# Moving the operands of TensorE by 64 bytes against the split weights, in a two-block transformer kernel

## The chip, the cores and the metric

One core of a Trainium2 chip runs the whole kernel. The time is the device time of one execution in microseconds (us); shown are medians of several runs, and one execution under the hardware profiler.

## What is computed

Two stacks of two layers each, on 256 tokens with 1024 features, in float32:

```
first block (256 latent and 256 context tokens, 512 in all):
  layer 0: modulated rmsnorm -> one projection to q, k, v and a gated branch
           -> neighbourhood attention + spatial gating -> projection -> residual
           rmsnorm -> conv FFN, inner width 2816 -> residual
  layer 1: the same frame with a retention mixer, then only the 256 latent tokens
second block (16 meta tokens + 256):
  layer 0: h + ab_mixer(rmsnorm(h))      # mLSTM and RG-LRU branches
           h + relu(rmsnorm(h) @ w1)^2 @ w2      # inner width 4096
  layer 1: h + differential attention, and the same MLP
  rmsnorm, without the 16 meta tokens
```

Nearly all of the arithmetic is `activations @ weights` with weight matrices that are each read once.

## The kernel before, in words

**Precision.** A float32 product is made of three fast passes. Every operand is split into a high part (rounded to the type float32r) and a low part (the rest). `project` (line 417) adds up high x high, low x high and high x low in PSUM; these are lines 456, 457 and 458. The activations are split where they are produced, by a norm or an activation function (`Hhi`/`Hlo`, `Fhi`/`Flo` and others); the weights are split as they arrive.

**Slots.** The weights come in slots of up to 1 MB (128 partitions x 2048 floats), listed in `PROJ`: `stream_weights` loads slot after slot from the sync queue into `w_raw[:, 0]` and `w_raw[:, 1]` in turn; ScalarE writes `w_hi` (`split_hi`, L383), VectorE writes `w_lo = w_raw - w_hi` (`split_lo`, L393), in two halves each; then TensorE uses the slot. Both have two buffers too, of 8 KB per partition, so one slot is prepared while the one before is used. The order of everything is written out by hand, with counted semaphores.

**Matmuls of a slot.** For most projections (`kind` "feat") the stationary operand is a 128 x 128 block of weights and the moving operand is one row of activations, that is 128 features x T tokens:

```
w = slice((k * p.C + c) * P, (k * p.C + c + 1) * P)
pe.matmul(o, w_hi[:, r, w], x_hi(k), start=k == 0, stop=False)
pe.matmul(o, w_hi[:, r, w], x_lo(k), start=False, stop=False)
mm = pe.matmul(o, w_lo[:, r, w], x_hi(k), start=False, stop=k == last)
```

T is 512 (`T1`) in layer 0 of the first block and in `ret_k`, 256 (`SEQ`) in the rest of its layer 1, in `c_outa`, `c_outb` and in the MLP of the last layer, and 272 (`T2`) in the rest of the second block. So a slot of 8 x 2 blocks is 48 matmuls, and one of 11 x 1 blocks (`ffn*_out*`) 33. For `kind` "tok" (`hyb_v*`, `ret_v`) the operands change places: 128 tokens of activations are stationary, 256 columns of weights move (lines 451 to 453). In the projections with a `fill` (`hyb_*`, `ret_g`, `ab_o`, `ab_gate`, `c_*`) small matmuls of the attention or of the recurrences stand between those of `project`.

**Which stages there are, and how many matmuls `project` issues in each:** `hyb_g` 96, `hyb_qk0` to `hyb_qk3` 48 each, `hyb_v0` and `hyb_v1` 96 each, `hyb_u` 96, `hyb_out` 192; `ffn0_in0` and `ffn0_in1` 528 each, `ffn0_out0` and `ffn0_out1` 264 each; `ret_k` 192, `ret_q` 192, `ret_v` 768, `ret_g` 384, `ret_out` 384; `ffn1_in0`, `ffn1_in1` 528 each, `ffn1_out0`, `ffn1_out1` 264 each; the `ab_*` stages 1584 in all; `mlp0_in0`, `mlp0_out0`, `mlp0_in1`, `mlp0_out1` 384 each; the `c_*` stages 768 in all; the four of `mlp1` 384 each. Together 11280 of TensorE's 13225 matmuls.

**Addresses.** All buffers are placed by hand (`at`, line 180 on): the address in a partition is `base` = 16512 plus the offset given. 16512 is 128 modulo 256. Modulo 256 the addresses before are: `w_hi` and `w_lo` 128 (each block of 512 bytes too); `X` 128; `Hhi512`, `Hhi256` and their `lo` 192, with rows of 2048 or 1024 bytes; `A`, the start of the working area, 64, and with it `Fhi512`, `Fhi256`, `rv_out` (moving operand of `ret_out`) and the outputs of the hybrid stage; `Hhi272` 128, `Fhi272` 64, `ABhi` 64, with rows of 1088 bytes = 4 x 256 + 64. The MLP of the last layer uses the 272 buffers with 256 columns of each row.

Of the kernel before, what the change touches and what calls it, by code (L numbers as in the profile page):

```python
# [171 lines left out]
def stack_kernel(nc, t, out, layers):  # L172
# [3 lines left out]
    with ctx:  # L176
# [92 lines left out]
        r_ctx = at("r_ctx", [P, 2, SEQ], A + 88 * KB)
        rq = at("rq", [P, 8, SEQ], A + 48 * KB)  # L270
        rg = at("rg", [P, 16, SEQ], A + 56 * KB)
        r_dist = at("r_dist", [P, 2, 2, SEQ], A + 72 * KB)
        r_dec = [at(f"r_dec{i}", [P, 4, SEQ], A + (76 + 4 * i) * KB) for i in range(2)]
        r_rope = at("r_rope", [P, 2, 2, SEQ], A + 80 * KB)
        r_e = at("r_e", [P, 2, SEQ], A + 84 * KB)
        r_rs = at("r_rs", [P, 2, SEQ], A + 86 * KB)
        r_sq = at("r_sq", [P, 2, SEQ], A + 90 * KB)
# [2896 lines left out]
```

## Time and profile before

| | |
|---|---|
| median of 3 runs | 2044.6 us (2042.35 to 2045.34) |
| the profiled execution, its own time | 2041.65 us |
| its span, first to last instruction | 2039.9 us |
| mean granted clock of TensorE | 0.983 |
| TensorE matmuls | 1938.5 us busy, 95%, 13225 |
| VectorE, ScalarE, GpSimd | 61%, 45%, 11% busy |
| HBM | 293.94 MB read, 145 GB/s over the span |

The profile is one execution. The busy time of TensorE is the union of its matmuls, which overlap: each lasts longer (in the records) than the distance to the start of the next. So the mean duration of a matmul is not what it costs; what it costs is the spacing of the starts, which is a stretch of time over the number of matmuls that start in it.

### The profile page before, as it was taken

The numbers are of one execution on the slowest core, as the hardware profiler recorded it, in microseconds if no ns is written. First come the engines' busy times: TensorE is split into PE (matmuls) and PEld (weight loads), VectorE is DVE, ScalarE is ACT, GpSimd is POOL, SyncE is SP. The second block draws the span as 40 slices with busy tenths as digits, with TensorE's granted clock in tenths as the row PEclk, the third lists the DMA queues.
The fourth block names the chain that finished last, engine by engine and source line by source line (L and its number), as shares of the span: only waits on it lengthen the run. The fifth ranks groups of instructions, "written<-read, shape, count | busy, mean of one in ns | idle before, by whom it ended". The sixth has DMA issues, their size and how long they took to land.

```text
span 2039.9 us, 33160 instructions
## 1 busy us (share of the span) xinstructions
PE 1938.5 (95%) x13225; PEld 1709.0 (84%) x13225; DVE 1251.0 (61%) x1853; ACT 920.6 (45%) x1438; POOL 217.7 (11%) x171
## 2 busy tenths in 40 slices
PE   4999989999999899999979998999999999989998
PEld 3776647778887479999979997998899999879997
DVE  6355466543654556678577767656975567787564
ACT  4344344322332242158465554347554444565353
POOL 2100104430542000011000000000010010000001
PEclk8999989999999899999999999999999999999999
DMA  8611464433222523223435544532444544224553
GB/s 357 229 69 63 164 228 165 167 125 111 83 90 85 206 83 128 101 83 104 145 136 170 208 162 142 174 137 83 139 171 167 177 174 145 94 94 170 186 182 124
DMA packets 43950, 296.78 MB, mean 145 GB/s; under 512 B 4976, under 2 KB 6128, under 8 KB 11696
## 3 DMA queue, kind: packets, MB, share of 16 engines
q1 hardware_dynamic: 36576, 247.48, 35.0%
q10 hardware_dynamic: 6048, 42.50, 5.9%
q0 software_dynamic: 1200, 5.02, 0.7%
q8 instruction: 90, 1.47, 0.3%
q14 instruction: 36, 0.29, 0.0%
HBM read 293.94 MB, written 1.05 MB: 145 GB/s over the span
## 4 chain that ended last, share of the span: by engine, by line
PE 83%; DVE 8%; ACT 4%; DMA 3%; issue 1%; POOL 1%; SPq 0%; ACTq 0%; DVEq 0%; POOLq 0%
PE acc L456 23%; PE acc L457 22%; PE acc L458 22%; DVE w_lo L393 2%; PE acc L451 2%; PE wk L550 2%; PE acc L453 2%; PE acc L452 2%; PE wk L1672 1%; DMA ada_first<-in_w_ada 1%; DMA ada_ring<-in_w_ada 1%; ACT w_hi L383 1%; PE wk L730 1%; PE acc L1661 1%; PE wk L1401 1%
## 5 line engine op out<-in xcount | busy, mean ns | idle before, releaser
L456 PE MATMUL acc<-Hhi,w_hi 128*128 128x272 f32 (+2 forms) x2304 | 740.5, 321 | 29.4 <-DVE Hlo L772 10.1
L457 PE MATMUL acc<-Hlo,w_hi 128*128 128x272 f32 (+2 forms) x2304 | 717.9, 312 | 0.0
L458 PE MATMUL acc<-Hhi,w_lo 128*128 128x272 f32 (+2 forms) x2304 | 717.5, 311 | 0.0
L393 DVE TENSOR_TENSOR w_lo<-w_raw,w_hi 128x1024 fp32r<-128x1024 f32 (+2 forms) x472 | 575.5, 1258 | 183.9 <-ACT w_hi L383 182.4
L383 ACT ACTIVATE w_hi<-w_raw 128x1024 fp32r<-128x1024 f32 (+2 forms) x472 | 452.3, 1005 | 432.9 <-PE acc L458 339.6
L456 PEld LDWEIGHTS acc<-Hhi,w_hi 128*128 128x128 f32 x2304 | 437.1, 190 | 79.7 <-issue 42.0
L457 PEld LDWEIGHTS acc<-Hlo,w_hi 128*128 128x128 f32 x2304 | 437.4, 190 | 22.1
L458 PEld LDWEIGHTS acc<-Hhi,w_lo 128*128 128x128 f32 x2304 | 436.5, 189 | 23.0
L456 PE MATMUL acc<-Fhi,w_hi 128*128 128x256 f32 (+2 forms) x864 | 265.1, 307 | 2.8 <-DVE w_lo L393 1.5
L458 PE MATMUL acc<-Fhi,w_lo 128*128 128x256 f32 (+2 forms) x864 | 264.6, 306 | 0.0
L457 PE MATMUL acc<-Flo,w_hi 128*128 128x256 f32 (+2 forms) x864 | 264.3, 306 | 0.0
L456 PEld LDWEIGHTS acc<-Fhi,w_hi 128*128 128x128 f32 x864 | 162.9, 189 | 12.6 <-issue 2.2
L458 PEld LDWEIGHTS acc<-Fhi,w_lo 128*128 128x128 f32 x864 | 162.7, 188 | 8.0
L457 PEld LDWEIGHTS acc<-Flo,w_hi 128*128 128x128 f32 x864 | 162.4, 188 | 7.9
L1047 ACT ACTIVATE cgu<-acc,vec 128x512 f32<-128x512 f32 x44 | 34.2, 779 | 127.6 <-PE acc L458 127.6
L451 PE MATMUL acc<-w_hi,Hhi 128*128 128x256 f32 x320 | 91.6, 286 | 0.0
L453 PE MATMUL acc<-w_hi,Hlo 128*128 128x256 f32 x320 | 88.7, 277 | 0.0
L452 PE MATMUL acc<-w_lo,Hhi 128*128 128x256 f32 x320 | 88.7, 277 | 0.0
L1069 DVE SCALAR_TENSOR_TENSOR cgu<-acc,vec,cgu 128x510 f32<-128x510 f32 x44 | 32.6, 743 | 90.5 <-ACT cgu L1047 90.5
L976 ACT ACTIVATE sq<-Y 128x512 f32<-128x512 f32 (+1 forms) x32 | 16.4, 523 | 120.9 <-DVE Y L958 61.1
L1906 DVE TENSOR_TENSOR X<-acc,X 128x272 f32<-128x272 f32 (+3 forms) x48 | 20.4, 434 | 75.1 <-PE acc L458 75.1
L958 DVE COPY Y<-acc 128x256 f32 (+3 forms) x32 | 17.9, 558 | 77.5 <-PE acc L458 77.4
(393 smaller groups left out, 2426.6 us busy)
## 6 DMA issues: line engine op xcount, KB each, us to landing
w_raw<-in_w_ffn_in SPq DMA_DIRECT2D x44, 1024.0 KB, 4.9
ada_ring<-in_w_ada ACTq DMA_DIRECT2D x40, 1024.0 KB, 4.9
w_raw<-in_w_mlp_in SPq DMA_DIRECT2D x32, 1024.0 KB, 4.9
w_raw<-in_w_mlp_out SPq DMA_DIRECT2D x32, 1024.0 KB, 4.9
w_raw<-in_w_ffn_out SPq DMA_DIRECT2D x32, 704.0 KB, 4.1
ada_first<-in_w_ada SPq DMA_DIRECT2D x8, 1024.0 KB, 18.4
w_raw<-in_w_ret_v SPq DMA_DIRECT2D x8, 1024.0 KB, 4.9
w_raw<-in_w_ret_g SPq DMA_DIRECT2D x8, 1024.0 KB, 4.8
```

Of the source, the lines that this page charges most:

```text
L383: act.activation(w_hi[:, r, a:b], w_raw[:, r, a:b], ACT.Copy).then_inc(hi_done, 1)
L393: dve.tensor_tensor(w_lo[:, r, a:b], w_raw[:, r, a:b], w_hi[:, r, a:b].bitcast(F32), ALU.subtract).then_inc(lo_done, 1)
L451: pe.matmul(o, x_hi(k)[:, toks], w_hi[:, r, w], start=k == 0, stop=False)
L452: pe.matmul(o, x_hi(k)[:, toks], w_lo[:, r, w], start=False, stop=False)
L453: mm = pe.matmul(o, x_lo(k)[:, toks], w_hi[:, r, w], start=False, stop=k == last)
L456: pe.matmul(o, w_hi[:, r, w], x_hi(k), start=k == 0, stop=False)
L457: pe.matmul(o, w_hi[:, r, w], x_lo(k), start=False, stop=False)
L458: mm = pe.matmul(o, w_lo[:, r, w], x_hi(k), start=False, stop=k == last)
L550: mm = pe.matmul(wk[b:b + 32, bank, 0:256], cvec[:, k, 30 - 2 * j:62 - 2 * j], w[:, k * 256:(k + 1) * 256], start=first and k < 4, stop=la ...
L1047: act.activation(cgu[:, r, c, 0:n], acc_tile(p, r, c), ACT.Identity, bias=Vd("conv_b", m + layer * 44), scale=Vd("conv_w", m + (layer * 3 ...
L1069: dve.scalar_tensor_tensor(seqs(o, 1, SEQ), seqs(acc_tile(p, r, c), 0, SEQ - 1), w, seqs(o, 1, SEQ), ALU.mult, ALU.add).then_inc(conv_left, 1)
L1906: ins = dve.tensor_tensor(x, acc_tile(p, st.parity(), c), x, ALU.add)
```

## The change

It changes addresses and one row length, and no instruction. `w_hi` and `w_lo` begin 64 bytes further (192 modulo 256). `X` and the `H` area move up by 256, `A` becomes a multiple of 256 (128 modulo 256 as an address). Then, modulo 256: `Hhi512`/`Hlo512` and `Fhi512`/`Flo512` and the hybrid's outputs lie at 128; `Hhi256`, `Fhi256`, `Fhi272` and `rv_out` at 192; `Hhi272` still at 128 and `ABhi` at 128 with rows of 1088 bytes. The rows of `Fhi272`/`Flo272` become 1152 bytes = 4 x 256 + 128. The norm ahead of the retention (j == 2) writes to `R_hi`/`R_lo`, rows of 512 tokens that begin at 192; `ret_k`, `ret_q`, `ret_v` and `ret_g` read them. The other buffers of the retention move by 64 against `A`.

```diff
-        w_hi = at("w_hi", [P, 2, SLOT], 16 * KB, F32R)
-        w_lo = at("w_lo", [P, 2, SLOT], 32 * KB, F32R)
-        X = at("X", [P, DC, T1], 48 * KB)
+        w_hi = at("w_hi", [P, 2, SLOT], 16 * KB + 64, F32R)
+        w_lo = at("w_lo", [P, 2, SLOT], 32 * KB + 64, F32R)
+        X = at("X", [P, DC, T1], 48 * KB + 256)
         HB = 4352 * 4
-        h0 = 64 * KB
+        h0 = 64 * KB + 256
...
-        A = (at_const[0] + 127) // 128 * 128 + 64
-
-        H_hi = {T1: at("Hhi512", [P, DC, T1], h0 + 64, F32R), SEQ: at("Hhi256", [P, 16, SEQ], h0 + 64, F32R),
+        A = (at_const[0] + 255) // 256 * 256
+
+        H_hi = {T1: at("Hhi512", [P, DC, T1], h0, F32R), SEQ: at("Hhi256", [P, DC, SEQ], h0 + 64, F32R),
                 T2: at("Hhi272", [P, 16, T2], h0, F32R)}
-        H_lo = {T1: at("Hlo512", [P, DC, T1], h0 + HB + 64, F32R), SEQ: at("Hlo256", [P, 16, SEQ], h0 + HB + 64, F32R),
+        H_lo = {T1: at("Hlo512", [P, DC, T1], h0 + HB + 256 + 0, F32R), SEQ: at("Hlo256", [P, DC, SEQ], h0 + HB + 256 + 64, F32R),
                 T2: at("Hlo272", [P, 16, T2], h0 + HB, F32R)}
+
+        R_hi, R_lo = at("Rhi", [P, DC, T1], h0 + 64, F32R), at("Rlo", [P, DC, T1], h0 + HB + 256 + 64, F32R)
...
-        F_hi = {T1: at("Fhi512", [P, FFH, T1], A + 16 * KB, F32R), SEQ: at("Fhi256", [P, FFH, SEQ], A + 16 * KB, F32R),
-                T2: at("Fhi272", [P, MLH, T2], A + 16 * KB, F32R)}
+        F_hi = {T1: at("Fhi512", [P, FFH, T1], A + 16 * KB, F32R), SEQ: at("Fhi256", [P, FFH, SEQ], A + 16 * KB + 64, F32R),
+                T2: at("Fhi272", [P, MLH, 288], A + 16 * KB + 64, F32R)}
...
-        rv_out = at("rv_out", [P, 4, 2048], A + 16 * KB, F32R)
+        rv_out = at("rv_out", [P, 4, 2048], A + 16 * KB + 64, F32R)
...
-                act.activation(H_hi[n][:, c, 0:n], n32[:, c % 2, 0:n], ACT.Copy).then_inc(hhi_ready, 1)
+                hi = R_hi if j == 2 else H_hi[n]
+                act.activation(hi[:, c, 0:n], n32[:, c % 2, 0:n], ACT.Copy).then_inc(hhi_ready, 1)
...
-            ret = (lambda k: H_hi[T1][:, k, LAT:T1], lambda k: H_lo[T1][:, k, LAT:T1])
-            project(pe, "ret_k", *hyb, need=h_need(pe, 2))
+            both = (lambda k: R_hi[:, k, :], lambda k: R_lo[:, k, :])
+            ret = (lambda k: R_hi[:, k, LAT:T1], lambda k: R_lo[:, k, LAT:T1])
+            project(pe, "ret_k", *both, need=h_need(pe, 2))
```

(`F_lo` changes as `F_hi` does, the low half of the norm as the high half, and `ret_v` takes `both` as well.)

## Rows read from the trace of the kernel before

**Rows 1.** The page: busy time by engine, and the chain that ended last
```profile
PE 1938.5 (95%) x13225; PEld 1709.0 (84%) x13225; DVE 1251.0 (61%) x1853; ACT 920.6 (45%) x1438; POOL 217.7 (11%) x171
...
PE 83%; DVE 8%; ACT 4%; DMA 3%; issue 1%; POOL 1%; SPq 0%; ACTq 0%; DVEq 0%; POOLq 0%
PE acc L456 23%; PE acc L457 22%; PE acc L458 22%; DVE w_lo L393 2%; PE acc L451 2%; PE wk L550 2%; PE acc L453 2%; PE acc L452 2%; PE wk L1672 1%; DMA ada_first<-in_w_ada 1%; DMA ada_ring<-in_w_ada 1%; ACT w_hi L383 1%; PE wk L730 1%; PE acc L1661 1%; PE wk L1401 1%
```

**Rows 2.** Waits of TensorE, longest first: us in total, times, longest
```profile
engine line waited for: us in total, times, longest us
PE wk L859 <- DVE sq_acc L899: 18.0, 1, 18.0
PE wk L550 <- DMA ada_ring<-in_w_ada: 12.1, 8, 3.1
PE acc L456 <- DVE Hlo L772: 10.1, 3, 4.5
PE acc L456 <- DVE Hlo L802: 7.8, 5, 5.6
...
PE acc L456 <- DVE w_lo L393: 4.2, 7, 0.9
```

**Rows 3.** Busy time by window, stretches of matmul behind matmul only
```profile
core 0: us, PE busy (x) PEld busy (x) DVE busy (x) ACT busy (x) POOL busy (x), PEclk, DMA share, GB/s
236.98:242.82 5.84, 5.84 (x27) 4.70 (x25) 0.90 (x2) 2.35 (x4) 1.49 (x2) 1.00 0.66 247
443.89:498.26 54.37, 54.37 (x235) 43.57 (x234) 17.38 (x21) 10.85 (x14) 0.00 (x0) 1.00 0.35 121
498.26:619.12 120.86, 120.86 (x530) 99.16 (x529) 68.47 (x64) 43.14 (x53) 55.49 (x30) 1.00 0.26 88
627.58:681.01 53.43, 53.43 (x231) 43.05 (x229) 19.89 (x22) 14.51 (x21) 7.11 (x6) 1.00 0.34 113
729.11:761.85 32.74, 32.74 (x144) 26.86 (x143) 12.33 (x14) 5.89 (x6) 0.00 (x0) 1.00 0.38 129
...
761.85:783.61 21.76, 21.76 (x193) 21.76 (x192) 12.75 (x16) 9.33 (x9) 0.00 (x0) 1.00 0.46 153
981.82:1021.16 39.34, 39.34 (x335) 39.34 (x335) 20.21 (x22) 16.23 (x21) 4.10 (x6) 1.00 0.56 187
1109.24:1135.33 26.09, 26.09 (x231) 26.09 (x231) 15.57 (x22) 10.05 (x14) 0.00 (x0) 1.00 0.65 220
1135.33:1197.52 62.19, 62.19 (x530) 62.19 (x529) 49.20 (x84) 38.11 (x62) 0.00 (x0) 1.00 0.51 176
1202.77:1229.74 26.97, 26.97 (x231) 26.97 (x230) 15.15 (x22) 13.01 (x21) 4.08 (x6) 1.00 0.62 209
1546.25:1594.67 48.42, 48.42 (x386) 48.42 (x385) 23.22 (x26) 17.16 (x18) 0.00 (x0) 1.00 0.49 175
1892.16:1937.59 45.43, 45.43 (x386) 45.43 (x385) 23.05 (x26) 17.11 (x18) 0.00 (x0) 1.00 0.54 185
```

**Rows 4.** TensorE by line and form: ret_q, ffn1_in1, ffn0_in1
```profile
line engine op names shapes xcount | busy us, mean ns | idle before us <-releasers
L456 PE MATMUL acc<-Hhi,w_hi 128*128 128x256 f32 x63 | 17.4, 276 | 0.0
...
L457 PE MATMUL acc<-Hlo,w_hi 128*128 128x256 f32 x171 | 47.9, 280 | 0.0
L458 PE MATMUL acc<-Hhi,w_lo 128*128 128x256 f32 x171 | 47.7, 279 | 0.0
...
L457 PE MATMUL acc<-Hlo,w_hi 128*128 128x512 f32 x168 | 66.2, 394 | 0.0
L456 PE MATMUL acc<-Hhi,w_hi 128*128 128x512 f32 x168 | 65.9, 392 | 0.0
L458 PE MATMUL acc<-Hhi,w_lo 128*128 128x512 f32 x168 | 65.2, 388 | 0.0
```

**Rows 5.** TensorE by line and form, 800 to 870 us, inside ret_v
```profile
L451 PE MATMUL acc<-w_hi,Hhi 128*128 128x256 f32 x191 | 53.9, 282 | 0.0
L453 PE MATMUL acc<-w_hi,Hlo 128*128 128x256 f32 x191 | 52.8, 276 | 0.0
L452 PE MATMUL acc<-w_lo,Hhi 128*128 128x256 f32 x191 | 52.8, 276 | 0.0
```

**Rows 6.** VectorE and ScalarE by line and form, whole execution
```profile
L393 DVE TENSOR_TENSOR w_lo<-w_raw,w_hi 128x1024 fp32r<-128x1024 f32 x400 | 507.5, 1308 | 159.6 <-ACT w_hi L383 158.6
...
L383 ACT ACTIVATE w_hi<-w_raw 128x1024 fp32r<-128x1024 f32 x400 | 400.7, 1049 | 384.1 <-PE acc L458 298.9 <-PE acc L453 77.1 <-DMA w_raw<-in_w_ffn_in 6.2
```

More of the change, by code:

```diff
@@ L231, in stack_kernel @@
         ada_ring = at("ada_ring", [P, 2, SLOT], nt0 + 18 * KB)
-        ada_rows = [at("ada_rows0", [P, 2, 256], A + 32 * KB), at("ada_rows1", [P, 1, 256], h0 + 16 * KB + 64)]
+        ada_rows = [at("ada_rows0", [P, 2, 256], A + 32 * KB), at("ada_rows1", [P, 1, 256], h0 + 16 * KB + 128)]
         sq2 = at("sq2", [P, 2, T2], A + 85 * KB)
@@ L239, in stack_kernel @@
         last = at("last", [P, DC, SEQ], h0)
-        F_hi = {T1: at("Fhi512", [P, FFH, T1], A + 16 * KB, F32R), SEQ: at("Fhi256", [P, FFH, SEQ], A + 16 * KB, F32R),
-                T2: at("Fhi272", [P, MLH, T2], A + 16 * KB, F32R)}
-        F_lo = {T1: at("Flo512", [P, FFH, T1], A + 38 * KB, F32R), SEQ: at("Flo256", [P, FFH, SEQ], A + 38 * KB, F32R),
-                T2: at("Flo272", [P, MLH, T2], A + 38 * KB, F32R)}
+        F_hi = {T1: at("Fhi512", [P, FFH, T1], A + 16 * KB, F32R), SEQ: at("Fhi256", [P, FFH, SEQ], A + 16 * KB + 64, F32R),
+                T2: at("Fhi272", [P, MLH, 288], A + 16 * KB + 64, F32R)}
+        F_lo = {T1: at("Flo512", [P, FFH, T1], A + 38 * KB, F32R), SEQ: at("Flo256", [P, FFH, SEQ], A + 38 * KB + 64, F32R),
+                T2: at("Flo272", [P, MLH, 288], A + 38 * KB + 64, F32R)}
         cgu = at("cgu", [P, 2, 2, T1], A + 60 * KB)
@@ L266, in stack_kernel @@
         ro = at("ro", [P, 8, 2, SEQ], A)
-        rv = at("rv", [P, 4, 2048], A + 16 * KB)
-        rv_out = at("rv_out", [P, 4, 2048], A + 16 * KB, F32R)
[L269 to L277, printed above, removed]
+        rv = at("rv", [P, 4, 2048], A + 16 * KB + 64)
+        rv_out = at("rv_out", [P, 4, 2048], A + 16 * KB + 64, F32R)
+        r_ctx = at("r_ctx", [P, 2, SEQ], A + 88 * KB + 64)
+        rq = at("rq", [P, 8, SEQ], A + 48 * KB + 64)
+        rg = at("rg", [P, 16, SEQ], A + 56 * KB + 64)
+        r_dist = at("r_dist", [P, 2, 2, SEQ], A + 72 * KB + 64)
+        r_dec = [at(f"r_dec{i}", [P, 4, SEQ], A + (76 + 4 * i) * KB + 64) for i in range(2)]
+        r_rope = at("r_rope", [P, 2, 2, SEQ], A + 80 * KB + 64)
+        r_e = at("r_e", [P, 2, SEQ], A + 84 * KB + 64)
+        r_rs = at("r_rs", [P, 2, SEQ], A + 86 * KB + 64)
+        r_sq = at("r_sq", [P, 2, SEQ], A + 90 * KB + 64)
         qk = at("qk", [P, 16, T2], A)
@@ L771, in lo @@
                 dve.wait_ge(hhi_ready, DC * j + c + 1)
-                dve.tensor_tensor(H_lo[n][:, c, 0:n], n32[:, c % 2, 0:n], H_hi[n][:, c, 0:n].bitcast(F32),
+                hi, lo = (R_hi, R_lo) if j == 2 else (H_hi[n], H_lo[n])
+                dve.tensor_tensor(lo[:, c, 0:n], n32[:, c % 2, 0:n], hi[:, c, 0:n].bitcast(F32),
                                   ALU.subtract).then_inc(h_ready, 1)
@@ L3002, in _ @@
             pe_ada_close(pe, ADA_RING)
-            ret = (lambda k: H_hi[T1][:, k, LAT:T1], lambda k: H_lo[T1][:, k, LAT:T1])
-            project(pe, "ret_k", *hyb, need=h_need(pe, 2))
+            both = (lambda k: R_hi[:, k, :], lambda k: R_lo[:, k, :])
+            ret = (lambda k: R_hi[:, k, LAT:T1], lambda k: R_lo[:, k, LAT:T1])
+            project(pe, "ret_k", *both, need=h_need(pe, 2))
             pe.wait_ge(s_mod, 9)
             project(pe, "ret_q", *ret)
-            project(pe, "ret_v", *hyb, after=lambda s: (all_freed(pe, "ret_q") if s == 0 else None,
+            project(pe, "ret_v", *both, after=lambda s: (all_freed(pe, "ret_q") if s == 0 else None,
                                                         pe_rope(pe, rope_items(), [2 * s, 2 * s + 1], SEQ, swap_ret, 0)))
```

## The prediction

> **What bounds the kernel now.** I read the page first. TensorE is busy 95% of the span, and the chain that ended last is 83% TensorE [rows 1]. The three matmul lines of `project` (L456, L457, L458) alone are 67% of that chain: for every row of activations one matmul with the high weights, one with the low activations, one with the low weights. The list of waits says how little stands between them: TensorE's longest wait is one of 18.0 us in the first norm, all its waits for L393's `w_lo` are 4.2 us, and the DMAs of the weights that `project` streams do not appear [rows 2]. So the time is a number of matmuls times the spacing of their starts, and the question is whether a new address changes a spacing.
>
> No row of the page gives a spacing, so I took stretches in which matmul follows matmul and divided their length by the matmuls that start in them (the count of the row, less one or two that are in flight at an edge; by the code 528 in `ffn0_in1`, 192 in `ret_q`, 384 in `mlp0_out0`) [rows 3]. 512 columns: 120.86/528 = 228.9 ns in `ffn0_in1`; 54.37/233 = 233.3 in `ffn0_out0` and 53.43/229 = 233.3 in `ffn0_out1`; 32.74/143 = 228.9 in `ret_k`; 5.84/25 = 233.6 in `hyb_out`. 256 columns: 21.76/192 = 113.3 in `ret_q`, 26.09/230 = 113.4 in `ffn1_out0`; 62.19/528 = 117.8 in `ffn1_in1`, 26.97/229 = 117.8 in `ffn1_out1`, 39.34/334 = 117.8 in `ret_out`; 45.43/384 = 118.3 in `mlp1_out0`. 272 columns: 48.42/384 = 126.1 in `mlp0_out0`. The granted clock is 1.00 (the 2.4 GHz level) in all of them, so it is not the clock. At one column a cycle they would be 213.3, 106.7 and 113.3 ns. The lines by form repeat it: a matmul of 256 columns lasts 276 ns in `ret_q` and 279 to 280 in `ffn1_in1`, one of 512 lasts 388 to 394 in `ffn0_in1` [rows 4].
>
> What differs between stretches of one width is where the moving operand lies against the weights. Addresses are the base of 16512 plus the offset; modulo 256 the weights lie at 128. `Hhi512` and `Hhi256` lie at 192: I call that distance 64. `Fhi` and the hybrid's outputs lie at 64: distance 192. Buffers with rows of 1088 bytes move on by 64 with every row: rotating. The 512-wide spacing follows the distance in every stretch: 228.9 at 64, 233.3 at 192. The 256-wide one holds one of two values at either distance (113.3 or 117.8), and 118.3 when it rotates. I take 113.3 (and 226.7, 120.4 in proportion to the columns) as the floor; the rest is a collision of the two reads of TensorE, the moving rows and the next weights. Other engines are hardly in it: `ret_q` stays on its floor with VectorE at work for 12.75 of 21.76 us.
>
> **Against that, a rule.** The measured fact is that 256 columns take 113.3 ns in one stretch and 117.8 in another at one clock [rows 3]. The Trainium skill, "SBUF — State Buffer", section "Who interferes with whom", says that PE and ACT never wait on anyone and gives the moving operand and the weight load a read port each; by it no placement matters and the sum below would be zero. The trace does not agree about the spacing, but it does not show that addresses are the cause either, since one distance has both values. So it stays a rival.
>
> **The change part by part.** No instruction, wait or DMA is added, removed or reordered. What changes is the distance. All counts are from the code.
>
> 1. Wide rows of the hybrid and of `ffn0_in` (96 + 192 + 96 + 1056 = 1440 matmuls): weights at 192, rows at 128, so distance 64 becomes 192. If only the distance counts they take on the spacing of `ffn0_out0`: 1440 x (233.3 - 228.9) = +6.3 us. Bound below: the floor, 1440 x (226.7 - 228.9) = -3.2. I take +6.3, since the nearest rows are the same instruction at that distance.
> 2. Wide rows of `hyb_out` and `ffn0_out` (720): 192 before and after, 0; bounds 720 x (226.7 - 233.3) = -4.8 and 0. `ret_k` (192) goes from 64 to 0, which no wide row shows: 0, bounds -0.4 and +0.8.
> 3. Narrow rows put at distance 0. `ffn1_in` 1056 at 117.8, `ret_g` and `ret_out` 768 at 117.8, `ffn1_out1` 264 at 117.8; `ffn1_out0` 264 and `ret_q` 192 are at the floor; `ret_v` (768, with weights as the moving operand) is there by its durations, 276 ns for two of its three lines (L451's 282 hold the restarts behind the rope matmuls) [rows 5]. No stretch stays at distance 0. Best: all on the floor, (1056 + 768 + 264) x 4.45 = -9.3. Worst that a steady stretch of this width shows: all at 117.8, so 264 x 4.4 = +1.2 for `ffn1_out0`, 192 x 4.5 = +0.9 for `ret_q`, 768 x (280 - 276) = +3.1 for `ret_v`: +5.2. I take -9.3: a fixed distance is the only thing found on the floor (in three stages of it), and the rotating rows never are. This is the weakest step.
> 4. `F` of the second block gets rows of 1152 bytes instead of 1088: the four distances become two, 0 and 128, in turn. Best -768 x (126.1 - 120.4) = -4.4 and -768 x (118.3 - 113.3) = -3.8, so -8.2; worst, as the rotation but without its better rows, +1. I take half of the best, -4.1.
> 5. `H272` still rotates over all four distances, only beginning at another: 0. `hyb_v` (192): 0. The split of the weights on ScalarE and VectorE, 1049 and 1308 ns for 1024 elements [rows 6], reads and writes other addresses: 0, because it is hidden behind the matmuls and TensorE waits 4.2 us in all for it. A slot of 48 matmuls lasts at least 5.4 us (48 x 113.3 ns), and its two halves keep VectorE for 2.6 and ScalarE for 2.1 us; if these became 10% slower it would be 0.3 us of that slack. A faster TensorE needs its weights sooner, but `ffn1_out0` runs on the floor while the DMA engines are at 0.65, so that cover holds [rows 3].
>
> Sum: +6.3 + 0 - 9.3 - 4.1 = -7.1 us. The profiled execution took 1.8 us more than its span, 2041.65, and lies 2.95 under the median of 2044.6; so 2034.5 for such an execution and **2037.5** for the median.
>
> **The rivals.**
> - *The wide rows gain as well.* Everything goes to the floor: -3.2 - 4.8 - 9.3 - 8.2 = -25.5, 2019.1 us. For it: the wide stages show matmuls of 388 ns among those of 392 and 394, so the floor exists there [rows 4]. Against: distance 192 is measured, at 233.3, in three stages.
> - *Slower: distance 192 for the wide rows, and no floor for the narrow.* The place is `ffn0_in` and the hybrid's input, the price +6.3, and it decides as soon as steps 3 and 4 give back less than 6.3 us, 47% of the 13.4 that I count on. With all narrow rows at 117.8 and step 4 at 0 it is +6.3 + 5.2 = +11.5, 2056.1 us. For it: `ffn1_in1`, `ffn1_out1` and `ret_out` sit at 117.8 at two different distances, so a fixed distance is no promise; if it is how a stage is entered that chooses, the floor of `ret_q` and `ffn1_out0` can be lost.
> - *No effect.* The spacing comes from something else that the addresses do not touch: 2044.6. For it: two values at one distance. Against: the wide rows keep 228.9 and 233.3 apart by distance without exception.
>
> **How the numbers follow.** A measurement of this kernel can tell about 0.2%, 4.1 us, from no change. Forecast (narrow rows gain, wide rows pay) 0.32; wide rows gain as well 0.18; no effect 0.13; slower 0.35; the last 0.02 is a balance of gain and loss inside 0.2%. Faster is the first two, 0.50; same 0.15; slower 0.35. The forecast's own range is 2033 (step 4 gives all of its 8.2) to 2046 (step 3 gives half, step 4 nothing). The range given takes in the slower case with the upper bounds of `ret_k` and step 4 (2056.1 + 0.8 + 1 = 2058) and reaches down to 2021, most of the way to the full gain at 2019; what lies beyond both ends is the rest of that rival and a few chances in a hundred above, together under 2 in 10.
>
> **What would show it.** In the changed profile the count of TensorE's matmuls is the same, 13225. Step 1: `ffn0_in1` at 233.3 ns (123.2 us for the stretch that took 120.86). Step 3: `ffn1_in1` at 113.3, 59.8 us for 62.19; `ret_g`'s durations 276 instead of 280. Step 4: `mlp0_out0` between 120.4 and 126.1, so 46.2 to 48.4 us, and `mlp1_out0` below 45.43. `ab_qk` at its old 126.1. The forecast is wrong if `ffn1_in1` stays at 62 us, if `ffn0_in1` is shorter than before, or if stretches of one stage and one distance change with no order.

## The result, and the profile after

The changed kernel takes 2058.9 us (median; 2056.9 to 2060.11), the kernel before 2044.26 beside it: ratio 1.0078, 95% interval 1.0064 to 1.0092 (the two medians alone give 1.0072). It is slower by 0.8%, outside the range given (2021 to 2058) and on the side of the rival "slower". The profiled execution took 2059.26 us with a span of 2057.5, 17.6 more than the span before.

The page of the changed kernel: busy time, and the chain that ended last (two source lines were added above `project`, so L456 to L458 are now L458 to L460). They answer to [rows 1].

```profile
PE 1957.9 (95%) x13225; PEld 1724.5 (84%) x13225; DVE 1252.9 (61%) x1853; ACT 921.3 (45%) x1438; POOL 217.7 (11%) x171
...
PE 84%; DVE 8%; ACT 4%; DMA 3%; issue 1%; POOL 1%; SPq 0%; DVEq 0%; ACTq 0%; POOLq 0%
PE acc L458 23%; PE acc L460 22%; PE acc L459 22%; DVE w_lo L395 2%; PE acc L453 2%; PE acc L455 2%; PE acc L454 2%; PE wk L552 2%; DMA ada_first<-in_w_ada 1%; PE wk L1676 1%; ACT w_hi L385 1%; DMA ada_ring<-in_w_ada 1%; PE wk L732 1%; PE acc L1665 1%; PE wk L1405 1%
```

TensorE is busy 19.4 us longer with the same 13225 matmuls; VectorE went from 1251.0 to 1252.9 us, ScalarE from 920.6 to 921.3. The waits of TensorE (us in total, times, longest) name the same causes as [rows 2], each within some 2 us of what it was, and the one for `w_lo` is a little shorter:

```profile
engine line waited for: us in total, times, longest us
PE wk L863 <- DVE sq_acc L903: 17.9, 1, 17.9
...
PE acc L458 <- DVE w_lo L395: 3.6, 6, 0.9
```

So nothing new is waited for, and the matmuls themselves stand further apart. Busy time by window, in the same stages as [rows 3] (stretch and its length, then busy time and count of each engine, granted clock, DMA share, GB/s); in order `ffn0_out0`, `ffn0_in1`, `ret_k`, `ret_q`, `ret_out`, and then `ffn1_out0`, `ffn1_in1`, `mlp0_out0`, `mlp0_in1`, `mlp1_out0`:

```profile
core 0: us, PE busy (x) PEld busy (x) DVE busy (x) ACT busy (x) POOL busy (x), PEclk, DMA share, GB/s
447.41:501.78 54.37, 54.37 (x234) 43.80 (x233) 17.36 (x21) 10.87 (x14) 0.00 (x0) 1.00 0.35 121
501.78:624.98 123.20, 123.20 (x529) 99.26 (x528) 68.34 (x64) 43.15 (x53) 55.36 (x30) 1.00 0.25 87
725.23:766.08 40.85, 40.85 (x181) 33.70 (x180) 18.69 (x27) 13.41 (x18) 0.00 (x0) 1.00 0.30 103
766.08:789.11 23.03, 23.03 (x193) 23.02 (x192) 12.75 (x16) 9.32 (x9) 0.00 (x0) 1.00 0.45 144
992.25:1032.32 40.07, 40.07 (x335) 40.07 (x335) 20.21 (x22) 16.22 (x21) 4.12 (x6) 1.00 0.54 185
...
1121.11:1148.71 27.60, 27.60 (x232) 27.60 (x231) 15.71 (x22) 10.04 (x14) 0.00 (x0) 1.00 0.60 208
1148.71:1212.07 63.36, 63.36 (x531) 63.36 (x530) 49.10 (x83) 38.11 (x62) 0.00 (x0) 1.00 0.49 173
1561.24:1609.88 48.64, 48.64 (x387) 48.64 (x386) 23.22 (x26) 17.16 (x18) 0.00 (x0) 1.00 0.49 173
1609.88:1658.30 48.42, 48.42 (x386) 48.42 (x385) 30.12 (x46) 23.74 (x30) 0.00 (x0) 1.00 0.51 175
1910.21:1955.44 45.23, 45.23 (x386) 45.23 (x385) 23.05 (x26) 17.12 (x18) 0.00 (x0) 1.00 0.53 186
```

Divided by the matmuls that start in them: `ffn0_in1` 123.20/528 = 233.3 ns (228.9 before), `ffn0_out0` 54.37/233 = 233.3 as before, `ret_k` 40.85/180 = 227.0 (228.9). And at 256 columns `ret_q` 23.03/192 = 120.0 (113.3), `ret_out` 40.07/334 = 120.0 (117.8), `ffn1_in1` 63.36/528 = 120.0 (117.8), `ffn1_out0` 27.60/230 = 120.0 (113.4). `mlp0_out0` 48.64/384 = 126.7 (126.1), `mlp1_out0` 45.23/384 = 117.8 (118.3), and `mlp0_in1`, whose rows still rotate, 48.42/384 = 126.1.

**Where the 17.6 us are.** For each stage I took the mean start-to-start time of the matmuls that follow one another without a pause, in both traces, and multiplied the difference by the stage's matmuls:

| part | matmuls | predicted, us | by measured spacing, us |
|---|---|---|---|
| 1. wide, distance 64 to 192 | 1440 | +6.3 | +5.8 |
| 2. wide, 192 to 192; `ret_k` 64 to 0 | 912 | 0 | -0.4 |
| 3. narrow, to distance 0 | 3312 | -9.3 | **+11.8** |
| 4. rows that alternate 0 and 128 | 1536 | -4.1 | +0.1 |
| 5. `hyb_v`, 64 to 192, and all the rest | 4080 | 0 | +0.3 |
| sum | 11280 | -7.1 | +17.6 |

That the sum is the difference of the spans to the digit is partly luck, because two things outside the table cancel. The pauses of the two norms ahead of `ffn0_in0` and `ret_k` are 2.3 us shorter in the changed execution, and `c_outa` and `c_outb` last 2.6 us longer. For `c_outb`, the kernel before and then the changed one:

```profile
1831.11:1843.97 12.86, 11.59 (x97) 11.42 (x97) 10.24 (x13) 6.58 (x12) 0.90 (x2) 1.00 0.62 220
1847.22:1861.98 14.76, 13.50 (x97) 13.32 (x97) 10.22 (x13) 6.98 (x12) 0.89 (x2) 0.86 0.53 189
```

That is the clock, 1.00 against 0.86, and it does not take the change: a second trace of the kernel before (`before_again`, below) has `c_outb` at 14.63 us and 0.86 as well, and its span, 2044.2, is only 13.3 us under the changed one. By the starts of the stages the changed execution is 15.4 us behind when `c_outa` begins, and the medians are 14.6 apart. So my estimate from these is that the addresses cost about 15 us, nearly all of it in the spacing of parts 1 and 3.

Nor do the other engines cause it, although their writes of `w_hi` and `w_lo` moved too: in `ffn1_in1` of the changed kernel all 527 spacings are 120 ns to the nanosecond of the trace, while VectorE is busy for 49.10 of the 63.36 us and ScalarE for 38.11, so a spacing is the same whether they are at work or not.

### The profile page after: what moved, and what is told of

The parts are those of the page before. It is cut to its first block, busy times and chain, and to the rows that moved or that the text cites. A ratio compares the mean times of both kernels' runs of the same rounds, so it can differ in the third digit from the quotient of the medians.

```text
span 2057.5 us, 33160 instructions
## 1 busy us (share of the span) xinstructions
PE 1957.9 (95%) x13225; PEld 1724.5 (84%) x13225; DVE 1252.9 (61%) x1853; ACT 921.3 (45%) x1438; POOL 217.7 (11%) x171
## 4 chain that ended last, share of the span: by engine, by line
PE 84%; DVE 8%; ACT 4%; DMA 3%; issue 1%; POOL 1%; SPq 0%; DVEq 0%; ACTq 0%; POOLq 0%
PE acc L458 23%; PE acc L460 22%; PE acc L459 22%; DVE w_lo L395 2%; PE acc L453 2%; PE acc L455 2%; PE acc L454 2%; PE wk L552 2%; DMA ada_first<-in_w_ada 1%; PE wk L1676 1%; ACT w_hi L385 1%; DMA ada_ring<-in_w_ada 1%; PE wk L732 1%; PE acc L1665 1%; PE wk L1405 1%
## 5 line engine op out<-in xcount | busy, mean ns | idle before, releaser
L458 PE MATMUL acc<-Hhi,w_hi 128*128 128x272 f32 (+2 forms) x2048 | 661.3, 323 | 25.4 <-DVE Hlo L776 7.9
L460 PE MATMUL acc<-Hhi,w_lo 128*128 128x272 f32 (+2 forms) x2048 | 643.3, 314 | 0.0
L459 PE MATMUL acc<-Hlo,w_hi 128*128 128x272 f32 (+2 forms) x2048 | 642.4, 314 | 0.0
L458 PEld LDWEIGHTS acc<-Hhi,w_hi 128*128 128x128 f32 x2048 | 391.5, 191 | 73.3 <-issue 39.8
L460 PEld LDWEIGHTS acc<-Hhi,w_lo 128*128 128x128 f32 x2048 | 391.3, 191 | 22.1
L458 PE MATMUL acc<-Fhi,w_hi 128*128 128x256 f32 (+2 forms) x864 | 265.9, 308 | 2.7 <-DVE w_lo L395 1.5
L460 PE MATMUL acc<-Fhi,w_lo 128*128 128x256 f32 (+2 forms) x864 | 265.2, 307 | 0.0
L458 PEld LDWEIGHTS acc<-Fhi,w_hi 128*128 128x128 f32 x864 | 162.8, 188 | 12.3 <-issue 2.2
L460 PEld LDWEIGHTS acc<-Fhi,w_lo 128*128 128x128 f32 x864 | 163.3, 189 | 8.0
L458 PE MATMUL acc<-Rhi,w_hi 128*128 128x256 f32 (+1 forms) x256 | 84.8, 331 | 2.3 <-DVE Rlo L776 2.3
L459 PE MATMUL acc<-Rlo,w_hi 128*128 128x256 f32 (+1 forms) x256 | 80.2, 313 | 0.0
L460 PE MATMUL acc<-Rhi,w_lo 128*128 128x256 f32 (+1 forms) x256 | 80.0, 312 | 0.0
L453 PE MATMUL acc<-w_hi,Rhi 128*128 128x256 f32 x256 | 73.7, 288 | 0.0
L454 PE MATMUL acc<-w_lo,Rhi 128*128 128x256 f32 x256 | 72.4, 283 | 0.0
L455 PE MATMUL acc<-w_hi,Rlo 128*128 128x256 f32 x256 | 72.4, 283 | 0.0
```

Source lines behind the costliest of these rows:

```text
L453: pe.matmul(o, x_hi(k)[:, toks], w_hi[:, r, w], start=k == 0, stop=False)
L454: pe.matmul(o, x_hi(k)[:, toks], w_lo[:, r, w], start=False, stop=False)
L455: mm = pe.matmul(o, x_lo(k)[:, toks], w_hi[:, r, w], start=False, stop=k == last)
```

## The experiments

Every run is of the whole kernel, with the change written in terms of addresses. Spacings in the text are a window's length over the matmuls that start in it, as above.

### The weights back, everything else as changed

```diff
-        w_hi = at("w_hi", [P, 2, SLOT], 16 * KB + 64, F32R)
-        w_lo = at("w_lo", [P, 2, SLOT], 32 * KB + 64, F32R)
+        w_hi = at("w_hi", [P, 2, SLOT], 16 * KB, F32R)
+        w_lo = at("w_lo", [P, 2, SLOT], 32 * KB, F32R)
```

> The changed kernel with w_hi and w_lo back at their old address (128 modulo 256); all else as changed. Theory (only the distance of the moving rows from the weights, modulo 256, sets the spacing): all stages of 512 columns are at distance 0 and take the 227.0 ns that ret_k shows after the change (ret_k itself, now at 64, 228.9); ffn1_in, ffn1_out, ret_q, ret_g and ret_out are at 64 and take 113.3 or 117.8 ns, not 120; hyb_v, now at distance 0, 120. Total 2160 x -6.4 ns and 3312 x -2.2 to -6.7 ns against the changed kernel: 2024 to 2038 us. Rival (the absolute address of a row sets it): spacings stay as in the changed kernel, 233.3 and 120, 2059 us. Rival (the address of the weights alone sets it): as in the kernel before, 228.9 and 233.3 at 512 columns.

Measured: 2036.7 us, ratio to the kernel before 0.9966 (0.9954 to 0.9979). Windows of its trace: `ffn0_out0`, `ffn0_in1`, `ffn0_out1`, `ret_k`, `ret_q`, `ffn1_in1`, `mlp0_out0`.

```profile
444.13:496.97 52.84, 52.84 (x235) 43.73 (x233) 17.36 (x21) 10.86 (x14) 0.00 (x0) 1.00 0.36 123
496.97:616.65 119.68, 119.68 (x530) 99.10 (x528) 68.35 (x64) 43.14 (x53) 55.28 (x30) 1.00 0.26 90
625.11:677.02 51.91, 51.91 (x231) 42.98 (x229) 19.85 (x22) 14.51 (x21) 7.08 (x6) 1.00 0.35 115
723.87:756.60 32.73, 32.73 (x144) 26.86 (x143) 12.32 (x14) 5.91 (x6) 0.00 (x0) 1.00 0.38 129
756.60:778.36 21.76, 21.76 (x193) 21.76 (x192) 12.75 (x16) 9.33 (x9) 0.00 (x0) 1.00 0.47 152
1131.06:1193.24 62.18, 62.18 (x530) 62.18 (x529) 49.03 (x83) 38.13 (x62) 0.00 (x0) 1.00 0.51 176
1541.41:1589.48 48.07, 48.07 (x386) 48.07 (x385) 23.21 (x26) 17.17 (x18) 0.00 (x0) 1.00 0.50 175
```

Row by row: 52.84/233 = 226.8 ns, 119.68/528 = 226.7, 51.91/229 = 226.7, 32.73/143 = 228.9, 21.76/192 = 113.3, 62.18/528 = 117.8, 48.07/384 = 125.2. No row of activations has moved against the changed kernel, yet each of these spacings has, those of the fixed rows to a value of their new distance: both rivals fall. The half of the change that places operands by width is worth 0.3% by itself; the 64 bytes of the weights turn it into a loss of 0.8%, by giving the wide rows the worst distance and the narrow ones theirs.

### The kernel before with only the weights moved, by 64, 128 and 192 bytes

```diff
-        w_hi = at("w_hi", [P, 2, SLOT], 16 * KB, F32R)
-        w_lo = at("w_lo", [P, 2, SLOT], 32 * KB, F32R)
-        X = at("X", [P, DC, T1], 48 * KB)
+        w_hi = at("w_hi", [P, 2, SLOT], 16 * KB + 64, F32R)
+        w_lo = at("w_lo", [P, 2, SLOT], 32 * KB + 64, F32R)
+        X = at("X", [P, DC, T1], 48 * KB + 256)
...
-        h0 = 64 * KB
+        h0 = 64 * KB + 256
```

and the same with 128 and with 192. (`X` and what lies behind it move by 256 to make room.)

> The kernel before with w_hi and w_lo 64 bytes further and nothing else (the buffers behind them move by 256, which changes no residue). Theory of the distance: the stages on Hhi go from 64 to 0: ffn0_in1 227.0 ns for 228.9, ffn1_in1 120.0 for 117.8, ret_q 120.0 for 113.3; the stages on Fhi and hyb_out go from 192 to 128, a distance not seen at 512 columns; mlp0_out0 stays at 126.1, since it rotates. Near 2050 us, give or take 4 for distance 128. Rival of the absolute row address: every spacing as before, 2044 us.

> The kernel before with w_hi and w_lo 128 bytes further. Theory of the distance: 64 and 192 change places, so ffn0_in1 goes from 228.9 to 233.3 ns and ffn0_out0 from 233.3 to 228.9; 256 columns stay at 113.3 or 117.8 in every stage, with no saying in which at which; about +7.2 - 3.2 = +4 us. Rival (the sign of the distance plays no part, or only modulo 128): nothing changes, 2044 us. Rival (weights at 0 modulo 256 are better or worse by themselves): all 512-column stages move the same way.

> The kernel before with w_hi and w_lo 192 bytes further. Theory of the distance: the stages on Hhi come to 128, not seen; those on Fhi, hyb_out and ret_out come to 0: ffn0_out0 and ffn0_out1 227.0 ns for 233.3, ffn1_out0, ffn1_out1 and ret_out 120.0. At 256 columns rows that alternate between 0 and 128 take 117.8, and 0 alone takes 120, so 128 should take less than 117.8, perhaps 113.3 to 116. Rival of the absolute row address: as before.

Measured: 2048.23 us (ratio 1.0029, 1.0018 to 1.0040), 2044.89 (1.0013, 1.0004 to 1.0022) and 2051.91 (1.0042, 1.0027 to 1.0058). With the weights 64 further, `ffn0_in1` (now distance 0), `ffn0_out1` (128) and `ffn1_in1` (0):

```profile
497.34:617.06 119.72, 119.72 (x529) 99.10 (x528) 68.34 (x64) 43.12 (x53) 55.31 (x30) 1.00 0.26 89
625.52:678.74 53.22, 53.22 (x231) 43.15 (x229) 19.86 (x22) 14.50 (x21) 7.08 (x6) 1.00 0.34 114
1140.99:1204.33 63.34, 63.34 (x530) 63.34 (x529) 49.06 (x83) 38.11 (x62) 0.00 (x0) 1.00 0.50 173
```

119.72/528 = 226.7, 53.22/229 = 232.4, 63.34/528 = 120.0 ns. With 128, `ffn0_in1` (192), `ffn0_out1` (64), `ffn1_in0` and `ffn1_in1` (192):

```profile
501.49:624.68 123.19, 123.19 (x529) 99.26 (x528) 68.34 (x64) 43.16 (x53) 55.34 (x30) 1.00 0.25 88
633.13:685.56 52.43, 52.43 (x230) 43.00 (x229) 19.89 (x22) 14.50 (x21) 7.11 (x6) 1.00 0.35 115
1064.38:1107.80 43.42, 43.42 (x384) 43.42 (x384) 37.76 (x67) 28.91 (x48) 0.00 (x0) 1.00 0.53 179
1140.14:1202.32 62.18, 62.18 (x530) 62.18 (x529) 49.04 (x83) 38.11 (x62) 0.00 (x0) 1.00 0.50 176
```

123.19/528 = 233.3 and 52.43/229 = 229.0: the two distances have changed places, and the sign matters. 43.42/383 = 113.4 and 62.18/528 = 117.8: the same stage form at the same distance, with both values in one execution. With 192, `ffn0_in1` (128), `ffn0_out1` (0), `ret_k` (128), `ret_q` (128), `ffn1_in1` (128), `ffn1_out1` (0):

```profile
501.00:624.20 123.20, 123.20 (x530) 99.11 (x529) 68.40 (x64) 43.12 (x53) 55.42 (x30) 1.00 0.25 88
632.73:684.65 51.92, 51.92 (x230) 42.98 (x229) 19.86 (x22) 14.51 (x21) 7.09 (x6) 1.00 0.35 115
723.06:765.12 42.06, 42.06 (x183) 34.10 (x181) 18.98 (x27) 13.65 (x19) 0.00 (x0) 1.00 0.29 100
765.12:787.90 22.78, 22.78 (x194) 22.78 (x193) 12.75 (x16) 9.32 (x9) 0.00 (x0) 1.00 0.44 146
1145.77:1208.43 62.66, 62.66 (x531) 62.66 (x529) 49.04 (x83) 38.10 (x62) 0.00 (x0) 1.00 0.50 174
1213.67:1241.15 27.48, 27.48 (x231) 27.48 (x231) 15.22 (x22) 13.12 (x21) 4.08 (x6) 1.00 0.62 205
```

123.20/528 = 233.3, 51.92/229 = 226.7, 42.06/181 = 232.4, 22.78/192 = 118.6, 62.66/528 = 118.7, 27.48/229 = 120.0. My guess for 256 columns at 128 (113.3 to 116) was wrong: it is 118.7. The rival of the absolute address is out in all three, since no row of activations changed its residue. Put together, ns per matmul:

| distance of the moving row from the weights, modulo 256 | 512 columns | 256 columns | 272 columns |
|---|---|---|---|
| 0 | 226.7 (`ret_k` 227.0 by its window, 226.7 once settled) | 120.0 | |
| 64 | 228.9 | 113.3 or 117.8 | 126.7 |
| 128 | 232.1 to 233.3 | 118.7 (120.0 in one stretch of `ret_v`) | |
| 192 | 233.3 | 113.3 or 117.8 | |
| alternating 0 and 128 | | 117.8 | 126.7 |
| alternating 64 and 192 | | 117.8 | 125.2 |
| rotating over all four | | 118.3 | 126.1 |

Wide rows are best at 0 and narrow ones worst there. The changed kernel puts most of its wide rows at 192, their worst, and its narrow ones at 0.

### A constant distance for the rows of 272

```diff
-                T2: at("Fhi272", [P, MLH, 288], A + 16 * KB + 64, F32R)}
+                T2: at("Fhi272", [P, MLH, 320], A + 16 * KB + 64, F32R)}
```

with the weights back, and the same for `Flo272`.

> after_w0 with rows of Fhi272 and Flo272 of 320 floats for 288, so that every row is at distance 64. mlp0_out0 and mlp0_out1 have shown 126.1 ns with rows that rotate over four distances, 126.7 alternating 0 and 128, 125.2 alternating 64 and 192. If it is constancy that allows the floor, 120.4 ns, or 124.7 in the upper of two states (118.0 + 6.7 in proportion); if the meeting at the row's end of 17 x 64 bytes counts, it stays at 125. mlp1_out0 and mlp1_out1 (256 columns) 113.3 or 117.8 for 117.8. Total 2029 to 2037 us against 2036.7.

Measured: 2037.54 us (0.9980, 0.9969 to 0.9991), about 1 us over the run without it. `mlp0_out0` and `mlp1_out0`:

```profile
1542.43:1591.07 48.64, 48.64 (x387) 48.64 (x385) 23.22 (x26) 17.17 (x18) 0.00 (x0) 1.00 0.48 173
1888.77:1934.00 45.23, 45.23 (x386) 45.23 (x385) 23.06 (x26) 17.12 (x18) 0.00 (x0) 1.00 0.52 186
```

48.64/384 = 126.7 and 45.23/384 = 117.8. Constancy does not give the floor at 272 columns, at least at distance 64, the only one tried; there it is worse than the alternation of 64 and 192. That a fixed distance by itself is good is the idea on which step 3 of the prediction rested, and it fails here too.

### Which two reads meet

The weights back, then `w_lo` alone 64 bytes further.

```diff
-        w_lo = at("w_lo", [P, 2, SLOT], 32 * KB, F32R)
+        w_lo = at("w_lo", [P, 2, SLOT], 32 * KB + 64, F32R)
```

> after_w0 with w_lo alone 64 bytes further. It asks which two reads meet. Theory (the moving rows of one matmul meet the load of the next one's weights): the load of w_lo goes on under the matmul before it, the one with the low activations, so of the three lines the second becomes longer at 512 columns; the three together go from 3 x 226.7 = 680 ns to 2 x 226.7 + 233.3 = 686.7, 228.9 a matmul, or 2 us more over the 2160 of them. Rival (the rows meet their own weights): the third line, high activations with low weights, becomes the longer one; the same sum. Rival (only w_hi counts, or the meeting is elsewhere): 226.7 stays. At 256 columns the theory gives the three a distance of 64, 0, 64, so a mean between 115.6 and 118.5 ns.

One execution, 2045.62 us. TensorE by line and form inside `ffn0_in1`, first the third line of the run with both at the old address, then the three of this one:

```profile
L460 PE MATMUL acc<-Hhi,w_lo 128*128 128x512 f32 x148 | 57.6, 389 | 0.0
...
L460 PE MATMUL acc<-Hhi,w_lo 128*128 128x512 f32 x144 | 57.2, 397 | 0.0
L459 PE MATMUL acc<-Hlo,w_hi 128*128 128x512 f32 x145 | 56.8, 392 | 0.0
L458 PE MATMUL acc<-Hhi,w_hi 128*128 128x512 f32 x145 | 56.4, 389 | 0.0
```

With both at the old address the three last 389 ns each; now the first still does, the second lasts 392 and the third, the one that multiplies by `w_lo`, 397. From the start of each to the next start it is 228.3, 229.1 and 235.9 ns, 693.3 for three, where both theories had 686.7. So most of the delay shows at the line that the rival named, some at the other two, and it is twice what either had. The span is 9.9 us over that of `after_w0`, where I had expected 2. At 256 columns `ret_q` and `ffn1_in1` took 117.8 on average, inside the 115.6 to 118.5 expected. It can be a meeting of the rows with their own weights, or one of the next load that shows a matmul later; this run does not say which, and it stays open. What it does say is that the address of one of the two weight buffers is enough to move the spacing.

### Is it the restart that chooses between 113.3 and 117.8?

The weights back, and one extra matmul between slots, the same in both runs; in the second the 256-wide rows of `ffn1` lie at distance 192 (offsets + 192 for + 64).

```diff
+            KICKS = ((4, 8, 16, 24, 32, 48, 64, 96, 128, 192), (12, 20, 28, 40, 56, 80, 112, 160, 256, 16))[half]
+
+            def kick(s):
+                if s < 10:
+                    m = KICKS[s]
+                    pe.matmul(wk[:, 2, 0:m], ones[:, :], one_row[:, 0:m], start=True, stop=True)
+            if layer == 1:
+                after_in = kick
```

> after_w0 with one extra matmul (4 to 256 columns of a constant, result unused) after each of the first ten slots of ffn1_in0 and of ffn1_in1, all at distance 64. In the traces so far 256 columns at a distance of 64 or 192 take 113.3 ns over a whole run of matmuls or 117.8 over a whole run, and change only where something stands between. Theory (the restart chooses): some of the 20 slots run at 113.3 and some at 117.8, by the length of what is put between. Rival (it belongs to the stage, or to the place of the buffers above 256 bytes): all 22 slots at 117.8 as in after_w0.

> The same 20 extra matmuls, with Hhi256, Hlo256, Fhi256 and Flo256 moved so that the distance is 192. By the theory of the restart again a mixture, perhaps at other lengths; ffn1_in0 was seen at 113.4 and at 117.8 at this distance. If neither this nor kick64 shows both values, the restart isn't what chooses.

(At distance 192 it was `ffn1_in0` that had been seen at 113.4 and `ffn1_in1` at 117.8, in the run with the weights 128 further.)

One execution each, 2043.58 and 2035.98 us. At distance 64 one of the 20 slots behind an extra matmul (the one behind 4 columns) ran at 113.3 and 19 at 117.8. At 192, 13 of 20 ran at 113.5 to 114.1 (113.3 once settled) and 7 at 117.8. Four consecutive slots of `ffn1_in1` in the second, behind 12, 20, 28 and 40 columns, from their second matmul to their last:

```profile
1135.72:1141.13 5.41, 5.41 (x47) 5.41 (x47) 3.91 (x7) 3.19 (x5) 0.00 (x0) 1.00 0.39 162
1141.59:1146.82 5.23, 5.23 (x47) 5.23 (x47) 4.05 (x7) 3.50 (x6) 0.00 (x0) 1.00 0.50 201
1147.28:1152.53 5.25, 5.25 (x47) 5.25 (x47) 4.25 (x8) 3.51 (x6) 0.00 (x0) 1.00 0.56 204
1152.99:1158.41 5.42, 5.42 (x48) 5.42 (x47) 4.41 (x9) 3.50 (x6) 0.00 (x0) 1.00 0.53 193
```

5.41 us for 46 or 47 starts against 5.23 and 5.25: the value changes at the restart and holds for the slot. In the ten traces with narrow rows at these distances that I went through, a run of matmuls without a pause settles within its first dozen and then keeps its value to its end; the one exception found is the last run of `ffn1_out1` in the version below, which took some 33 matmuls to settle. That the program alone doesn't decide it shows in the kernel before, traced once more:

> The kernel before once more, for a second trace. The question is whether 113.3 or 117.8 at 256 columns and a distance of 64 or 192 belongs to the program or to the execution. after_w0, f320, kick64 and kick192 are the same program up to ret_q, and ret_q took 113.3 ns in the first and 117.8 in the others; so by theory at least one stage differs from the first trace of this kernel (ret_q at 117.8, or ffn1_out0 at 117.8, or another at 113.3), while 228.9, 233.3 and 126.1 stay to 0.1 ns. Rival: all stages as before to 0.1 ns.

2046.01 us. `ffn0_in1`, `ret_q`, `ret_out`:

```profile
499.32:620.18 120.86, 120.86 (x530) 99.17 (x528) 68.43 (x64) 43.13 (x53) 55.35 (x30) 1.00 0.26 88
762.93:785.54 22.61, 22.61 (x193) 22.61 (x192) 12.75 (x16) 9.32 (x9) 0.00 (x0) 1.00 0.45 147
987.87:1023.25 35.38, 35.38 (x315) 35.38 (x313) 17.52 (x19) 13.92 (x18) 3.70 (x5) 1.00 0.55 192
```

120.86/528 = 228.9 again to the last digit, but `ret_q` 22.61/192 = 117.8 where it had been 113.3 [rows 3], and `ret_out` 35.38/312 = 113.4 where it had been 117.8. So which of the two a stage gets is not fixed by the program and can differ between executions, which is part of the spread of this kernel's runs. What decides it at a restart stays open.

### A version that beats both

The weights back; the 256-wide rows of `ret_out` and `ffn1` at distance 192; the last MLP gets buffers of its own with rows of 1024 bytes at 192 (`M_hi`, `M_lo` for the normed input, `N_hi`, `N_lo` for the hidden rows).

```diff
+        M_hi = at("Mhi", [P, DC, SEQ], h0 + 192, F32R)
+        M_lo = at("Mlo", [P, DC, SEQ], h0 + HB + 192, F32R)
+        N_hi = at("Nhi", [P, MLH, SEQ], A + 16 * KB + 192, F32R)
+        N_lo = at("Nlo", [P, MLH, SEQ], A + 38 * KB + 192, F32R)
```

> after_w0 with the rows of 256 columns at distance 192 in ret_out, ffn1 and also in the last MLP, which gets rows of 1024 bytes of its own in place of the rotating ones. Theory: mlp1_in0 to mlp1_out1 leave 118.3 and 117.8 for 113.3 or 117.8; which one is chance of the restart, so 2036.7 us less 0 to 16. Rival: 118.3 in the last MLP came from its place and not from its rotation, and stays.

Measured: 2026.9 us, ratio 0.9908 (0.9892 to 0.9923). `ffn1_in1` and `mlp1_in1`:

```profile
1126.93:1186.77 59.84, 59.84 (x531) 59.84 (x529) 49.51 (x84) 38.11 (x62) 0.00 (x0) 1.00 0.52 183
1925.82:1971.05 45.23, 45.23 (x386) 45.23 (x385) 29.64 (x46) 23.36 (x30) 0.00 (x0) 1.00 0.55 187
```

`ffn1_in1` is on the floor for all its 528 matmuls, 59.84 us (62.18 in the run with distance 64); the long runs of the other three stages of `ffn1` and of `ret_out` were there too. The last MLP took 117.8 in all four: better than rotating, not the floor. Then with one extra matmul of 24 columns early in nine stages, and in the last MLP alone:

```diff
+            at_slot = {"ret_out": 1, "ffn1_in0": 1, "ffn1_out0": 1, "ffn1_in1": 0, "ffn1_out1": 1,
+                       "mlp1_in0": 1, "mlp1_out0": 1, "mlp1_in1": 0, "mlp1_out1": 1}.get(name)
+            if at_slot is not None:
+                after = lambda s: pe.matmul(wk[:, 2, 0:24], ones[:, :], one_row[:, 0:24], start=True, stop=True) \
+                    if s == at_slot else None
```

> narrow192 with one extra matmul of 24 columns after slot 0 or 1 of nine stages (ret_out, four of ffn1, four of mlp1). In kick192 lengths of 16 to 32 columns were followed by 113.3 ns in all six slots that had them. Theory (such a restart at distance 192 always falls into the lower state): the nine stages at 113.3 to 113.5, that is 1056 x 4.4 + 912 x 4.4 + 768 x 5.0 + 768 x 4.4 ns = 16 us less than after_w0, less 9 x 0.1 for the extra matmuls: near 2022 us, 1.0% under the kernel before. Rival (chance): some of the nine at 117.8, so 2024 to 2034.

> narrow192 with the extra matmuls only in the four stages of the last MLP, where all four were followed by 113.4 ns in kicked. Theory (there the restart at distance 192 falls into the lower state): mlp1_in0 to mlp1_out1 at 113.4, 1536 x 4.4 = 6.7 us less than narrow192: near 2020 us, 1.1% under the kernel before. Rival (chance, by execution): some of the four at 117.8, and a median between 2020 and 2027. ffn1 and ret_out without extra matmuls at either value.

Measured: 2029.12 us (0.9926, 0.9912 to 0.9939) and 2030.01 (0.9942, 0.9927 to 0.9956). In the first, `ffn1_in0` and `mlp1_out0`; in the second, `ffn1_in1`, `c_outb` and `mlp1_out0`:

```profile
1051.69:1096.80 45.11, 45.11 (x385) 45.11 (x384) 38.07 (x67) 28.48 (x48) 0.00 (x0) 1.00 0.49 173
1893.21:1925.77 32.56, 32.56 (x289) 32.56 (x288) 16.69 (x18) 11.92 (x12) 0.00 (x0) 1.00 0.54 193
```

```profile
1131.89:1191.73 59.84, 59.84 (x530) 59.84 (x529) 48.88 (x84) 38.01 (x62) 0.00 (x0) 1.00 0.54 184
1824.21:1838.85 14.64, 13.37 (x98) 13.20 (x97) 10.24 (x13) 6.98 (x12) 0.90 (x2) 0.86 0.55 189
1896.76:1929.32 32.56, 32.56 (x288) 32.56 (x288) 16.70 (x18) 11.98 (x12) 0.00 (x0) 1.00 0.55 193
```

The last MLP went to 32.56/287 = 113.5 in both, as expected, but in the first run `ffn1_in0` (45.11/383 = 117.8) and both `ffn1_out` stages went up, six of nine stages being low. "This length always falls low" is refuted. In the second the longest unbroken run of every stage of `ffn1` and of the last MLP was low, and the profiled execution was still no shorter than that of the version without extra matmuls (spans 2028.3 and 2027.7). By the starts of the stages in both traces the last MLP gave back 5.7 us of the 6.7 expected, and stages without a change took it again. 1.8 us of that is the clock: `c_outb` took 14.64 us at a mean granted clock of 0.86, where it took 12.86 at 1.00 in the other. 1.4 us is `ret_out`, which drew 117.8 here and 113.3 there; 1.5 is `ffn1_in0` and 2.7 lies ahead of `ret_out`, both not taken apart. So the extra matmuls do what they were put in for in the last MLP, but no gain in the whole time was measured. In the last MLP alone they are above the version without them (the intervals of the ratios do not meet); in nine stages the intervals overlap, 0.9892 to 0.9923 and 0.9912 to 0.9939. The version without them has the lowest median.

## Why the prediction was wrong

**What held.** That the time is matmuls times spacing, that the change acts on the spacing alone, and that the distance of moving row and weights modulo 256 decides it: four places of the weights against the old rows and two against the new gave every long stretch a value of its distance; the narrow rows at 64 and 192 have a choice of two there, and the wide rows at 128 vary by 1.2 ns. Step 1 took the spacing of `ffn0_out0` for rows that come to its distance, and `ffn0_in1` came to 233.3 exactly; +5.8 us against +6.3, since the stages whose matmuls are broken up by others were slowed less. That the delay is a collision of the moving rows with the load of the next weights, as the prediction has it, was not shown; the run that moved `w_lo` alone leaves open which two reads meet. Steps 2 and 5 held. The cover of the weights' split held (3.6 us of waits).

**The step that failed is step 3**, "a fixed distance is the only thing found on the floor (in three stages of it), and the rotating rows never are". It took the good value from distances 64 and 192 and gave it to distance 0, of which no stretch existed. At 0 the 256-wide matmul takes 120.0 ns, in every stage and every run, above both values that I used as bounds. So the term was +11.8 us, not -9.3, and my "worst that a steady stretch of this width shows", +5.2, was not a bound but the second of two states at other distances. The rotating rows did contain distance 0 and were no help either: in `mlp1_in1` of the kernel before, the three matmuls of a row at distance 0 start 118.1 ns apart, and not the 120.0 of a steady stretch, so what a row costs in turn with others does not tell what it costs alone.

**Step 4** failed in the same way on a smaller scale: +0.1 for -4.1. Alternating 0 and 128 cost 0.6 ns at 272 columns and gave 0.5 back at 256.

**The rival that came true** was "slower: distance 192 for the wide rows, and no floor for the narrow", at chance 0.35. Its price for the wide rows was right. Its sum, +11.5, is short of the +17.6 of the table by 6.1, and that is part 3: +11.8 where the rival, with 117.8 as the worst, had +5.2. That its 2056.1 comes as near as 2.8 us to 2058.9 is partly luck, since the execution traced before was 2.6 us under its median and had `c_outb` at the full clock. Against it I had set "a fixed distance holds the floor", with the counter-evidence in the same rows: three stages at a fixed distance sat at 117.8.

**The rule weighed against the trace.** The Trainium skill ("SBUF — State Buffer", "Who interferes with whom") has it that PE never waits on anyone, with a port each for moving operand and weight load. The runs don't agree that the two are independent of each other: moving the two weight buffers by 64 bytes, with not one instruction changed, took the wide matmul from 233.3 to 226.7 ns and the narrow one from 120.0 to 113.3 or 117.8. The two values at one distance, which I had counted for "no effect", change, in the traces here, only where the run of matmuls is restarted.

## What to carry to other kernels

Where matmul follows matmul and each has its own weights, compare the spacing of starts with columns over clock, stage by stage, and tabulate it by the residues of both operands before moving any of them; a distance that no stage shows can be bought with one run in which only the weights move. A value seen at one distance says nothing about the next, and two widths can want opposite ones. Before two single traces are compared to a microsecond, compare the stages that were not changed: one dip of the clock in `c_outb` was worth 1.8 us here. A layout that is better for one stage is only half of a placement: here the half by width was worth 0.3%, and a shift of the weights on top of it cost 1.1%.
